# Second attention of a float32 network: plain float32 scores in row halves, k projected first, part of the rotary work on GpSimd

## The reference, cut to what matters

```
def gqa_attention(h, w_qkv, q_g, k_g, w_o, cos, sin):
    qkv = h @ w_qkv
    q, k, v = jnp.split(qkv, [Q_WIDTH, Q_WIDTH + KV_WIDTH], axis=-1)
    q = apply_rope(rmsnorm(q.reshape(B, T, N_HEADS, HEAD_DIM), q_g), cos, sin)
    k = apply_rope(rmsnorm(k.reshape(B, T, N_KV_HEADS, HEAD_DIM), k_g), cos, sin)
    v = v.reshape(B, T, N_KV_HEADS, HEAD_DIM)
    ...
        s = jnp.einsum('bqkgd,bskd->bkgqs', q_blk, k).astype(jnp.float32) * scale
        p = jax.nn.softmax(s, axis=-1).astype(v.dtype)
        return jnp.einsum('bkgqs,bskd->bqkgd', p, v)
    ...
    return o @ w_o
```

## Time and profile before

| | |
|---|---|
| median of three runs | 3081.43 us (3077.9 to 3084.54) |
| the profiled execution's own time | 3084.61 us |
| its span, first to last instruction | 3082.8 us |
| TensorE busy | 2848.1 us (92%) |
| VectorE, ScalarE, GpSimd busy | 1363.7, 1083.8, 1141.5 us |
| projection to attention (stretch from 1600 to 1707.5) | 107.5 us |
| attention (stretch from 1707.5 to 1820) | 112.5 us |

### The profile page before, as it was taken

How to read it: one execution, slowest core, us unless ns; L and a number is a source line. 1 busy time by engine, 2 the same in 40 slices (tenths; PEclk the granted TensorE clock), 3 DMA queues, 4 the chain that set the end, 5 groups by cost and what they waited for, 6 DMA issues and landing times.

```text
span 3082.8 us, 37081 instructions
## 1 busy us (share of the span) xinstructions
PE 2848.1 (92%) x13438; PEld 2323.6 (75%) x13438; DVE 1363.7 (44%) x1533; ACT 1083.8 (35%) x1509; POOL 1141.5 (37%) x466
## 2 busy tenths in 40 slices
PE   7998799999989998999967898999989988989999
PEld 6786577778867767778855677888878876878887
DVE  4323738775273447776345555122220145331232
ACT  4322234333333333334333544233344222432332
POOL 3442043444424113344422004445434434434443
PEclk9998799999989999999988999999999999999999
DMA  5331025663322104763222002333323331323232
GB/s 146 89 95 55 14 86 186 213 190 102 96 76 86 30 28 142 220 217 123 89 62 65 1 15 82 96 94 96 96 82 101 108 99 48 96 77 99 91 96 75
DMA packets 314313, 297.67 MB, mean 97 GB/s; under 512 B 11932, under 2 KB 246632, under 8 KB 314088
## 3 DMA queue, kind: packets, MB, share of 16 engines
q1 hardware_dynamic: 299784, 235.64, 25.7%
q10 hardware_dynamic: 14432, 60.70, 5.9%
HBM read 294.21 MB, written 2.10 MB: 96 GB/s over the span
## 4 chain that ended last, share of the span: by engine, by line
PE 46%; issue 34%; POOL 13%; DVE 5%; ACT 2%; POOLq 0%; DMA 0%; ACTq 0%; DVEq 0%
POOL wlo L514 13%; PE ps L1758 8%; PE ps L1760 8%; PE ps L1759 8%; PE ps L1673 6%; PE ps L1674 6%; PE ps L1675 6%; DVE nrm L1446 1%; DVE rowst L1414 1%; PE ps L1938 1%; DVE gk L1573 1%; PE ps L1911 0%; ACT pbuf L800 0%; PE ps L1784 0%; PE ps L1786 0%
## 5 line engine op out<-in xcount | busy, mean ns | idle before, releaser
L514 POOL TENSOR_TENSOR wlo<-raw,whi 128x1024 fp32r<-128x1024 f32 x444 | 1118.0, 2525 | 1882.6 <-ACT whi L546 1882.5
L1673 PE MATMUL ps<-xhi,whi 128*128 128x512 f32 x1824 | 714.6, 392 | 22.2 <-POOL wlo L514 20.7
L1674 PE MATMUL ps<-xlo,whi 128*128 128x512 f32 x1824 | 710.7, 390 | 0.0
L1675 PE MATMUL ps<-xhi,wlo 128*128 128x512 f32 x1824 | 710.6, 390 | 0.0
L546 ACT ACTIVATE whi<-raw 128x1024 fp32r<-128x1024 f32 x444 | 465.3, 1049 | 278.2 <-PE ps L1760 199.3
L1758 PE MATMUL ps<-whi,ahi 128*128 128x512 f32 x1184 | 465.7, 393 | 18.2 <-issue 15.1
L1760 PE MATMUL ps<-whi,alo 128*128 128x512 f32 x1184 | 463.6, 392 | 0.0
L1759 PE MATMUL ps<-wlo,ahi 128*128 128x512 f32 x1184 | 463.6, 392 | 0.0
L1673 PEld LDWEIGHTS ps<-xhi,whi 128*128 128x128 f32 x1824 | 342.9, 188 | 104.3 <-POOL wlo L514 32.0
L1675 PEld LDWEIGHTS ps<-xhi,wlo 128*128 128x128 f32 x1824 | 342.8, 188 | 71.6
L1674 PEld LDWEIGHTS ps<-xlo,whi 128*128 128x128 f32 x1824 | 342.9, 188 | 70.2
(11 more groups left out here) (266 smaller groups left out, 3121.1 us busy)
## 6 DMA issues: line engine op xcount, KB each, us to landing
adaraw<-in_ada_w ACTq DMA_DIRECT2D x64, 768.0 KB, 5.7
raw<-in_ffn_w_up SPq DMA_DIRECT2D x88, 512.0 KB, 3.8
raw<-in_mlp_w_in SPq DMA_DIRECT2D x64, 512.0 KB, 4.0
raw<-in_mlp_w_out SPq DMA_DIRECT2D x64, 512.0 KB, 3.7
raw<-in_gmlp_w_in SPq DMA_DIRECT2D x48, 512.0 KB, 3.8
raw<-in_sc_ssm_w_in SPq DMA_DIRECT2D x44, 512.0 KB, 3.8
raw<-in_ffn_w_down SPq DMA_DIRECT2D x44, 512.0 KB, 3.7
raw<-in_fox_w_in SPq DMA_DIRECT2D x24, 512.0 KB, 3.7
```

The costliest lines, as they stand in the source:

```text
L514: pool.tensor_tensor(wlo[:, j], raw[:, j], whi[:, j].bitcast(F32), ALU.subtract).then_inc(w_lo, 1)
L1673: pe.matmul(out, lh, rh, start=start, stop=False)
L1674: pe.matmul(out, lh, rl, start=False, stop=False)
L1675: return pe.matmul(out, ll, rh, start=False, stop=stop)
```

## The change

The scores are made in plain float32 from unsplit q and k. q of two heads lies in the upper and lower 64 rows of `qT` (a head pair p), k twice in both halves of `kT`; a step has four matmuls of 64 rows by 256 keys, alternating between the row halves, each half writing a bank of its own. `qsp`, `ksp`, `qS`, `kS`, `kL`, `roped` and the splits are gone; builds are one for a head pair: four of k, two of q ahead of the attention, six of q inside it.

The projection's order becomes k and v, first q half, second q half. Between the third and fourth unit of the last part TensorE makes the k transposes. VectorE does the rotary work of k and of the first q half. The second q half is copied by ScalarE to `q1raw`; GpSimd squares it, VectorE sums it inside the attention (ahead of the maximum of step 3), ScalarE takes the root (ahead of the exponentials of step 4), VectorE the reciprocal (step 5), and GpSimd does the 20 rotary steps. Its first user is the build of head pair 4 at the end of step 12. The weight split of the output projection's fourth unit follows this on GpSimd.

In the second attention each step's transposes are copied half by ScalarE and half by VectorE, with a semaphore count for each half. The first block's attention keeps its operations.

```diff
-        sp_t(sp, "qkv", w_qkv, 4, [0, HALF, D])
+        sp_t(sp, "qkv", w_qkv, 4, [D, 0, HALF])
...
+        def rope_q1():
+            n = 0
+
+            def step(ins):
+                nonlocal n
+                ins.then_inc(q1_step, 1)
+                n += 1
+
+            heads8 = lambda x: x.rearrange("p (h d) -> p h d", d=HD)
+            pair = lambda x: x.rearrange("p (h d e) -> p h d e", d=HD // 2, e=2)
+            for t in range(NT):
+                pool.wait_ge(q1_copied, t + 1)
+                pool.tensor_tensor(sqb[:, t], q1raw[:, t], q1raw[:, t], ALU.mult).then_inc(q1_sq, 1)
+            pool.wait_ge(q_sum, 15)
+            for t in range(NT):
+                tabs = gcs[:, 0, t, 1].rearrange("p (d e) -> p d e", e=2)
+                if t:
+                    pool.wait_ge(q1_step, n)
+                step(pool.tensor_tensor(heads8(qn[:]), heads8(q1raw[:, t]),
+                                        hsum[:, 2, t].unsqueeze(2).to_broadcast([P, 8, HD]), ALU.mult))
+                pool.wait_ge(q1_step, n)
+                step(pool.tensor_tensor(heads8(ra[:]), heads8(qn[:]),
+                                        gcs[:, 0, t, 0].unsqueeze(1).to_broadcast([P, 8, HD]), ALU.mult))
+                for e in range(2):
+                    step(pool.tensor_tensor(pair(rb[:])[:, :, :, e], pair(qn[:])[:, :, :, 1 - e],
+                                            tabs[:, :, e].unsqueeze(1).to_broadcast([P, 8, HD // 2]), ALU.mult))
+                pool.wait_ge(q1_step, n)
+                step(pool.tensor_tensor(qr[:, t, 8:16], heads8(ra[:]), heads8(rb[:]), ALU.add))
+            assert n == Q1_STEPS
+
+        turn = END["qkv"] // RING
+        assert END["qkv"] % RING == 0 and U0["go"] % RING == 0
         with pool.Fori(0, turn) as i:
             for j in range(RING):
                 lo_part(i * RING + j, j)
+        for j in range(RING - 1):
+            lo_part(END["qkv"] + j, j)
+        rope_q1()
+        lo_part(END["qkv"] + RING - 1, RING - 1)
...
-            if w >= 0 and w % 2 == 0:
+            if w >= 0 and (A or w % 2 == 0):
                 N = (w % 4 + 1) * P if causal else T
-                act.wait_ge(at_tp, G + w + 1)
+                act.wait_ge(at_tp, B + 2 * w + (1 if A else 2))
                 if w >= 4:
                     act.wait_ge(at_pv, G + w - 3)
                 z = 2 * w % TSLOTS
-                act.activation(ptb[:, z:z + 2, 0:N], ps[:, TBANK:TBANK + 2, 0:N], ACT.Copy).then_inc(at_pt_a, 1)
+                if A:
+                    act.activation(ptb[:, z, 0:N], ps[:, TBANK, 0:N], ACT.Copy).then_inc(at_pt_a, 1)
+                else:
+                    act.activation(ptb[:, z:z + 2, 0:N], ps[:, TBANK:TBANK + 2, 0:N], ACT.Copy).then_inc(at_pt_a, 1)
...
+        for j in range(K_BUILDS):
+            act.wait_ge(bd_tp, j + 1)
+            act.activation(kT[:, j], ps[:, j], ACT.Copy).then_inc(bd_ev_a, 1)
+        act.wait_ge(unit_done, END["qkv"])
         for t in range(NT):
+            act.activation(q1raw[:, t], ps[:, 4 + t], ACT.Copy).then_inc(q1_copied, 1)
+
+    def act_q1_std(act):
+        act.wait_ge(q_sum, 14)
+        act.activation(hsum[:, 1], hsum[:, 0], ACT.Sqrt, scale=1.0 / HD, bias=eps_ln[:, 1:2]).then_inc(q_std, 1)
+
+    def act_build_at(act, g):
+
+        p = g // 4 + 1
+        if g % 4 == 0 and Q_FIRST <= p < 8:
+            act.wait_ge(bd_tp, K_BUILDS + p + 1)
+            act.activation(qT[:, p], ps[:, RBANK], ACT.Copy, scale=HD ** -0.5).then_inc(bd_ev_a, 1)
...
+                if A:
+                    dve.tensor_copy(ptb[:, z + 1, 0:N], ps[:, TBANK + 1, 0:N]).then_inc(at_pt_d, 1)
+                else:
+                    dve.tensor_copy(ptb[:, z:z + 2, 0:N], ps[:, TBANK:TBANK + 2, 0:N]).then_inc(at_pt_d, 1)
...
+                if hh:
+                    step(dve.tensor_tensor(qr[:, t, 0:8], v3(ra), v3(rb), ALU.add))
+                else:
+                    twice = lambda x: v3(x).unsqueeze(2).to_broadcast([P, 4, 2, HD])
+                    step(dve.tensor_tensor(kr[:, t], twice(ra), twice(rb), ALU.add))
+        assert n == 40
+        for p in range(Q_FIRST):
+            dve.wait_ge(bd_tp, K_BUILDS + p + 1)
+            dve.tensor_scalar(qT[:, p], ps[:, 2 + p], HD ** -0.5, None, ALU.mult).then_inc(bd_ev_d, 1)
+
+    def dve_q1_sums(dve):
+        for t in range(NT):
+            dve.wait_ge(q1_sq, t + 1)
+            dve.tensor_reduce(hsum[:, 0, t], sqb[:, t].rearrange("p (h d) -> p h d", d=HD), AX.X, ALU.add
+                              ).then_inc(q_sum, 1)
+
+    def dve_q1_rstd(dve):
+        dve.wait_ge(q_std, 3)
+        dve.reciprocal(hsum[:, 2], hsum[:, 1]).then_inc(q_sum, 1)
...
+    def scores_gqa(pe, g):
+        p, i = divmod(g, 4)
+        if g == 1:
+            pe.wait_ge(bd_ev_d, Q_FIRST)
+        if g == LAG:
+            pe.wait_ge(q1_copied, 4)
         if i == 0:
+            pe.wait_ge(bd_ev_d, min(p + 1, Q_FIRST))
+            pe.wait_ge(bd_ev_a, max(K_BUILDS, K_BUILDS + p + 1 - Q_FIRST))
+        for c in range(2):
+            for b in range(2):
+                r, n = slice(64 * b, 64 * b + 64), slice(256 * c, 256 * c + 256)
+                ins = pe.matmul(ps[:, 2 * (g % 2) + b, n], qT[r, p, i * P:(i + 1) * P], kT[r, p // 2, n],
+                                start=True, stop=True)
+        return ins
+
+    def pe_qkv(pe):
+
+        S = U0["qkv"]
+
+        def units(h, js):
+            for j in js:
+                pe_t_unit(pe, S + 4 * h, j, j, 4 * ((h + 1) % 2), xhi[:, 2 * j:2 * j + 2], xlo[:, 2 * j:2 * j + 2], j == 0)
+
+        pe.wait_ge(res_add, 32)
+        units(0, range(4))
+        pe.wait_ge(xt_ev, 40)
+        units(1, range(4))
+        pe.wait_ge(q_step, 5 * 3 + 1)
+        pe.wait_ge(v_ev, 4)
+        units(2, range(3))
+        pe.wait_ge(q_step, 20 + 5 * 3 + 1)
+        for h in range(4):
+            for t in range(NT):
+                ins = pe.transpose(ps[:, h, t * P:(t + 1) * P], kr[:, t, h].rearrange("p b d -> p (b d)"), ident)
+            ins.then_inc(bd_tp, 1)
+        units(2, [3])
+        pe.wait_ge(q_step, 40)
+        for p in range(Q_FIRST):
+            if p == 0:
+                pe.wait_ge(bd_ev_a, K_BUILDS)
+            pe_build_q(pe, p, 2 + p)
+
+    def pe_build_q(pe, p, bank):
         for t in range(NT):
+            ins = pe.transpose(ps[:, bank, t * P:(t + 1) * P], qr[:, t, 2 * p:2 * p + 2].rearrange("p b d -> p (b d)"), ident)
         ins.then_inc(bd_tp, 1)
 
     def pe_build_at(pe, g):
 
+        p = g // 4 + 1
+        if g % 4 == 0 and Q_FIRST <= p < 8:
+            if p > Q_FIRST:
+                pe.wait_ge(at_rc, 8 + p - Q_FIRST)
+            if p >= 4:
+                pe.wait_ge(q1_step, Q1_STEPS)
+            pe_build_q(pe, p, RBANK)
```

More of the change, by code:

```diff
@@ L76 @@
     _n += 2 * _k
[L79 to L89, removed]
+K_BUILDS, Q_FIRST, Q1_STEPS = 4, 2, 20
 def host_constants():
@@ L520, in _ @@
                 lo_part(i * RING + j, j)
+        for j in range(RING - 1):
+            lo_part(END["qkv"] + j, j)
+        rope_q1()
+        lo_part(END["qkv"] + RING - 1, RING - 1)
+        with pool.Fori(turn + 1, U0["go"] // RING) as i:
+            for j in range(RING):
+                lo_part(i * RING + j, j)
+        turn = U0["go"] // RING
         for j in range(RING - 1):
@@ L791, in act_attn @@
         for g in range(32 + LAG):
-            if g == 28 and hook:
-                hook()
+            if hook:
+                hook(g)
             if g < 32:
@@ L1032, in _, with beside @@
         act_qkv(act)
-        act_attn(act, 1, ptb2, False, hook=lambda: (act.wait_ge(at_o, 12), act_first_splits(act, oT2)),
-                 build=lambda g: act_build(act, BUILD_AT[g]) if g in BUILD_AT else None)
+        def beside(g):
+            if g == 4:
+                act_q1_std(act)
+            if g == 28:
+                act.wait_ge(at_o, 12)
+                act_first_splits(act, oT2)
+        act_attn(act, 1, ptb2, False, hook=beside, build=lambda g: act_build_at(act, g))
         for s, (name, src) in enumerate((("o", oT2), ("md0", hid_mlp), ("go", uT), ("md1", hid_mlp))):
@@ L1408, in dve_attn @@
         for g in range(32 + LAG):
-            if g == 29 and hook:
-                hook()
+            if hook:
+                hook(g)
             if g < 32:
@@ L1473, in dve_qkv @@
         dve.wait_ge(q_tab, 6)
-        for hh in range(3):
-            nh = 4 if hh == 2 else 8
+        for hh in range(2):
+            b0, nh = (4, 4) if hh == 0 else (0, 8)
             w = nh * HD
@@ L1904, in weigh @@
             pr, i = divmod(g, 4)
[L1905 removed]
+            if A:
+                pe.wait_ge(at_pt_a, 16 + g + 1)
+                pe.wait_ge(at_pt_d, 16 + g + 1)
+            else:
+                pe.wait_ge(at_pt_d if g % 2 else at_pt_a, g // 2 + 1)
             if i == 0 and pr:
@@ L1927, in pe_attn @@
                     pe.wait_ge(at_exp, B + 2 * g - 2)
-                for b in range(2):
```

(13 more changed lines are left out.)

157 lines of the change are left out of this document (43 added, 114 removed).

## The result

The changed kernel takes 3049.41 us, median of four runs (3048.69 to 3049.8), against 3079.73 us (3077.9 to 3084.54) for the kernel before on the same chip: a ratio of 0.9899, 95% interval 0.9882 to 0.9916. Its profiled execution took 3049.15 us, so 35.5 us less than the one of before, while the medians lie 30.3 us apart. On another chip, seven runs of the kernel before and four of the changed one gave 3083.55 and 3049.03 us, which is 34.5 us apart (ratio 0.9892, 0.9875 to 0.9908).

A forecast was written before the change was run, and what follows sets the result against it. TensorE's waits were taken as the bound: VectorE's chain behind the projection before the attention, a ring over three engines within it. 3084.6 - 37.5 + 1.8 = 3048.9, less 3.2: 3046 us predicted, range 3040 to 3061.

The forecast's parts named there:

- The sum: Whole kernel: 3084.6 - 37.5 + 1.8 = 3048.9 us in the profiled execution's terms; less 3.2, predicted 3046 us.
- The likeliest case: Whole kernel: row halves overlap in the scores and GpSimd's rotary work is in time; 3041 to 3051 us, chance 0.70.
- The start: Projection to first scores: k's earlier place removes waits, scores start at about 1670.0 and not 1707.51; gain 37.5 us.
- the start does not move: Before the attention: VectorE-GpSimd meetings or late weights delay k's transposes 1 to 3 us; chance 0.04, shared with dearer table loads.
- The scores: Attention: eight plain float32 passes a step, row halves overlapping, end after 1.07 us, else after 1.71.
- the rival: Attention scores: row halves do not overlap, 4.2 us a step against 3.70; 14 us less 1, 3059 us; chance 0.12.
- The ring: Attention's loop over three engines: 7.3 to 7.5 us a pair of steps against 7.40, neither gain nor loss.
- The insertions: Attention, steps 3 to 8: VectorE's sums and ScalarE's root cost 5.4 us gross, loss 1.8 us.
- GpSimd: Attention: second q half's rotary work takes 21 us, ends before step 12's end with 9 us of cover, costs nothing.

The follow-up runs named there:

- the half-array kernel: Changed kernel with all four score matmuls of a step on the lower 64 rows, the upper rows left out: 3066.91 us, ratio 0.9953.
- the doubled work: Changed kernel with each token tile of the second q half turned twice on GpSimd, 40 rotary steps and not 20: 3062.46 us, ratio 0.9941.

## Why the prediction was right, step by step

**The sum.** In the profiled execution's terms 3048.9 was predicted and 3049.15 measured. The likeliest case came: halves overlap, GpSimd in time. That the sum fits to 0.3 us is luck in part. The start gave 36.1 us and not 37.5, the attention cost 0.7 and not 1.8; the rest has no term in the sum: this execution reached the projection 1.2 us sooner and was 1.2 us longer behind the attention.

**The start.** Scores were predicted 70 us after about 1600 and came 72.2 after the projection's start, at 1670.2 as forecast, though TensorE had begun 1.2 us before the start of the kernel before. The size that was off is the k transposes: the banks were expected free 2.3 us early, and TensorE waited 1.32 us for them. The cover was enough for one meeting of VectorE with GpSimd; three occurred in the q half, two of them (2.77, 2.04 us, 3.4 us more than twice 0.69) ahead of the fourth first-step, which ended at 1661.48 and not 1658.9. That is the rival "the start does not move", in its mild form. The order q, k and v, q takes this wait away and gives 1.6 us, which shows it.

**The scores.** Overlap was right, its picture was not. I had a first and a last pass stand alone, 5 pass lengths and 1.19 us with the shape changes. Passes start in pairs, so it is four lengths of 0.213 and 0.11 more between the first pair and the second: 0.97 from the first step's scores to the second's, 1.06 with a shape change behind. Scores to maximum took 1.18 (1718.48 to 1719.66), not 1.39. In series they cost 17.2 us (the half-array kernel), where the rival said 14 less 1.

**The ring.** 7.28 us a pair, at the low edge of 7.3 to 7.5. It hides two errors that partly cancel: scores that were shorter than put down, and half copies that I had put down as a saving (0.72 us instead of 1.17). The copy is shorter, but it stands in ScalarE's queue in every step, and the half copies as a whole cost 4 us.

**The insertions.** They were put down as a loss of 1.8 us in steps 3 to 8. The starts of the scores in both traces show where the attention lost. Step 8's scores start 26.27 us after the first scores, and 26.20 before: the rest of the change makes up there for what root and sums cost. Steps 8 to 24 gain 1.0 us (58.3 against 59.3). From the scores of step 24 to those of step 31 it is 26.2 us against 24.6, a loss of about 1.6 us that the sum has no term for. With whole copies it is 24.9, so most of this loss is the half copies. The root alone costs 0.9, as its removal shows; what the sums alone cost was not measured.

**GpSimd.** 21 us predicted, 21.9 measured; 9 us of cover predicted, 8 measured, by the changed kernel and by the doubled work. Broadcast operands cost nothing extra: 1.04 and 1.27 us against 1.31 assumed, and 1.27 for the plain sum. A half product on every second element took 0.83 us against 0.7 assumed; no row shows a plain operation of that size, so what the operands have to do with it stays open. The weight split behind it waited for ScalarE, not for the rotary work.

**The step that failed** is the last: taking 3.2 us off because the profiled execution of before was 3.2 above its median. That was a property of one execution, not of the profile. All executions of before lie between 3075.1 and 3084.6, and the profiled one was the slowest; the changed kernel's eight timed runs lie between 3048.65 and 3050.09 with the profiled one in their middle. So 3046 is 3.4 us too low, and nearly all of it is this term. The measured gain depends on the runs of before in the same way: it is 30.3 us by four of them, 34.5 by seven others, where 35.4 was forecast. Part of the scatter sits ahead of the projection, which profiled executions reached between 1590.3 and 1599.2, while start and attention repeated within 0.1 us (72.2 and 120.4 in the second profile of the changed kernel). Why executions of some kernels scatter by 9 us and of others by 1.5 stays open.

## What to carry to other kernels

When a chain of small vector work decides when a stage starts, order the projections so that the part with the longest chain behind it is not last, and hand what isn't needed at once to an idle engine with its cover counted in microseconds. A copy split over two engines is done only when the later queue has come to its half: in this ring, whole copies by the two engines in turns were 4 us faster, so measure both. Compare stages by their own length in the trace, and don't carry one execution's distance to the median over to another kernel.

## What the hardware showed that was not expected

- With matmuls of 64 rows on both row halves, passes start in pairs about 0.01 us apart and run side by side, in plain float32 too, in both orders of issue that were measured. Eight passes of 256 columns hold the queue 1.06 us, four of 512 columns 1.05, and eight in one half 1.92.
- With all score matmuls on the same 64 rows, a weight load of 0.187 us for each pass costs nothing beside passes of 0.21 us.
- A VectorE operation of 0.69 us on SBUF tiles that met GpSimd's split took 2.04 to 2.85 us, three times in one part of 20 operations, and each time it ended 0.55 us behind the end of the split. An operation that reads the banks took its usual 0.69 us in the middle of a split (`qn` at 1656.59), and during the attention, with GpSimd's rotary work beside them, the row maxima stayed at 1.22 us.
- After a wait of 13 to 16 us TensorE ran at or near the lower clock level for some microseconds in all three kernels that had one: the granted clock was 0.50 in the 8 us about the end of the wait with the rotary work on VectorE, 0.59 in the 4.3 us behind it with GpSimd's work doubled, 0.50 from 1678.1 to 1684.3 with k last. The kernel before shows the same behind its waits of 7.57 and 11.11 us: the granted clock was 0.51 and 0.55 there, and 16 transposes took 3.68 us where the changed kernel's 16 take 1.97. So some 4 of the 36 us at the start are the clock, an estimate from these 16 and the 32 behind them (6.59 us against twice 1.97).
